# A norm's row kept on chip, keys and mask loaded later, and an output gain moved from VectorE to ScalarE's copy

## The reference

```
proj  = rms_norm(x) * norm_mix_g @ w_in            # recurrent group | q | k | v
y_r   = rwkv7_group(proj[..., :P_RWKV], ...)       # 8 heads x 64, delta-rule recurrence
o     = windowed attention over 2 chunks of history, softmax with a sink per head
y_a   = o * rsqrt(mean(o * o per head) + eps) * out_g            # attn_out_g, 512 values
x     = x + concat(y_r, y_a) @ w_out
t     = x * rsqrt(mean(x * x) + eps) * norm_ffn_g                # the second norm, 1024 values
# per row and head (8): scores with 2 x 128 keys, best 16 of the 16 x 16 sums, then
x     = x + sum over 128 experts of gate * gelu(down[e] . t) * up[e]
y     = rms_norm(x) * norm_final_g
```

## Time and profile before

| | before |
|---|---|
| median of 3 runs | 3971.74 us (3968.76 to 3976.06) |
| the profiled execution, its own time | 4006.36 us |
| its span, first to last instruction | 4004.6 us |
| mean granted clock of PE | 0.867 |
| busy share of PE, DVE, POOL, ACT | 78%, 72%, 38%, 35% |
| moved by DMA | 1424.83 MB, 356 GB/s over the span |
| of it the gathers' queue | 1223.91 MB |

### The profile page before, as it was taken

How to read it: one execution, slowest core, us unless ns; L and a number is a source line. 1 busy time by engine, 2 the same in 40 slices (tenths; PEclk the granted TensorE clock), 3 DMA queues, 4 the chain that set the end, 5 groups by cost and what they waited for, 6 DMA issues and landing times.

```text
span 4004.6 us, 43462 instructions
## 1 busy us (share of the span) xinstructions
PE 3116.8 (78%) x13880; PEld 1785.9 (45%) x13880; DVE 2889.2 (72%) x6010; ACT 1403.7 (35%) x4013; POOL 1534.6 (38%) x1323
## 2 busy tenths in 40 slices
PE   7999977778777877787778777877787778776556
PEld 4655645445443545354526353635363536352112
DVE  2221468779778886988698869886978698868775
ACT  2111133524343443334333524352425242523223
POOL 1333133334333433443344333442433244325554
PEclk9999988888798879887988798889878987899679
DMA  7234379999899999999999999999999999999998
GB/s 260 99 124 158 107 319 386 419 369 368 336 417 380 387 371 415 375 386 372 418 386 363 395 417 356 380 408 406 378 361 386 414 364 383 402 380 397 420 420 350
DMA packets 243305, 1424.83 MB, mean 356 GB/s; under 512 B 27763, under 2 KB 53107, under 8 KB 95606
## 3 DMA queue, kind: packets, MB, share of 16 engines
q0 software_dynamic: 170784, 1223.91, 75.6%
q1 hardware_dynamic: 61222, 180.44, 11.8%
q10 hardware_dynamic: 11072, 17.70, 1.3%
HBM read 1389.02 MB, written 34.17 MB: 355 GB/s over the span
## 4 chain that ended last, share of the span: by engine, by line
PE 31%; DVE 28%; DMA 12%; ACT 9%; issue 6%; POOL 1%; another core or an unknown queue 1%; DVEq 0%; POOLq 0%; PEldq 0%; SPq 0%; ACTq 0%
DVE ex_rows L1607 12%; PE mx_ps L1593 11%; DMA ex_rows<-experts,mx_expert 6%; PE mx_ps L1257 4%; DVE mx_acc L1617 2%; DMA mx_xs<-w_q 2%; DMA mx_fac<-w_q 2%; DMA mx_ex<-w_out 2%; PE mx_ps L1035 2%; ACT L1563 1%; PE mx_ps L1042 1%; PE mx_ps L999 1%; PE mx_ps L1240 1%; PE mx_ps L1038 1%; ACT L756 1%
## 5 line engine op out<-in xcount | busy, mean ns | idle before, releaser
L1552 POOL DMA_INDIRECT ex_rows<-experts,mx_expert x1152 | 1406.0, 1220 | 2084.1 <-PE mx_ps L1593 1202.6
L1593 PE MATMUL mx_ps<-ex_rows,ex_diag 128*128 128x512 f32 x2740 | 1506.1, 696 | 400.9 <-ACT ex_diag L1573 385.1
L1607 DVE CUSTOM_DVE_ANT_0 ex_rows<-ex_rows,mx_acc 128x1024 f32<-128x1024 f32 x1152 | 1371.8, 1221 | 151.8 <-DMA ex_rows<-experts,mx_expert 133.7
L1593 PEld LDWEIGHTS mx_ps<-ex_rows,ex_diag 128*128 128x128 f32 x2740 | 564.7, 219 | 1169.0 <-issue 1161.5
L1563 ACT ACTIVATE ex_coef<-ex_coef 128x1 f32<-128x1 f32 x1152 | 213.7, 200 | 1463.8 <-DVE ex_coef L1607 1450.1
L1617 DVE SCALAR_TENSOR_TENSOR mx_acc<-ex_rows,ex_coef,mx_acc 128x1024 f32<-128x1024 f32 x467 | 599.0, 1283 | 92.5 <-ACT ex_coef L1566 64.8
L1416 PE MATMUL mx_ps<-pj_w,pj_hT 128*128 128x432 f32 x768 | 292.5, 539 | 5.8 <-ACT mx_acc L1429 4.7
L1566 ACT ACTIVATE ex_coef<-ex_coef,mx_gate 128x1 f32<-128x1 f32 x1152 | 283.9, 284 | 10.6
L1573 ACT ACTIVATE ex_diag<-cn_ident,ex_coef 128x128 f32<-128x128 f32 x685 | 255.5, 394 | 10.7
L1416 PEld LDWEIGHTS mx_ps<-pj_w,pj_hT 128*128 128x128 f32 x768 | 146.8, 194 | 138.2 <-issue 135.5
L1563 ACT ACT_TABLE_LOAD x130 | 166.8, 1283 | 13.4 <-DVE ex_coef L1607 10.4
(11 more groups left out here) (316 smaller groups left out, 3978.9 us busy)
## 6 DMA issues: line engine op xcount, KB each, us to landing
mx_fac<-w_q SPq DMA_DIRECT2D x54, 512.0 KB
mx_ex<-w_out SPq DMA_DIRECT2D x36, 512.0 KB
mx_ex<-w_q SPq DMA_DIRECT2D x36, 512.0 KB
ex_rows<-experts,mx_expert POOLq DMA_INDIRECT x1152
mx_p_cur<-w_q SPq DMA_DIRECT2D x27, 512.0 KB
mx_xs<-w_q SPq DMA_DIRECT2D x27, 512.0 KB
proj_rows<-mx_acc ACTq DMA_DIRECT2D x48, 216.0 KB, 1.9
mx_fac<-w_out SPq DMA_DIRECT2D x18, 512.0 KB
```

The source lines that it names most:

```text
L1552: pool.indirect_dma_start(rows[:, g % RING, :], None, A["experts"], bass.IndirectOffsetOnAxis(expert[:, t % 2, s:s + 1], 0))\
L1593: last = pe.matmul(bank(6 + c), diag[:, diags.due(t, n) % DIAGS, :], up[:, r, c * 512:(c + 1) * 512], start=n == 0, stop=n == len(on_pe(t) ...
L1607: dve.tensor_tensor_reduce(out=down[:, r, :], in0=down[:, r, :], in1=tn[:, :], scale=1.0, scalar=0.0, op0=ALU.mult, op1=ALU.add, accum_out ...
```

## The change

The row of the second norm becomes a constant on chip: it is loaded once in `prepare` into a buffer of its own, and `route_sync` no longer loads it. The keys, values and mask of a prompt tile are loaded into the buffer `bkT`, after the last product that reads it, by `queries_sync` instead of `mix_sync`; their two buffers go. The gain of attention's output is no longer a row that DVE multiplies with: it is loaded as a 128 x 4 column table, and ACT applies it as a scale in its copy of the transposed `cat`, where a column of the output is a partition.

```
-    for name, at, n in (("r_k", RKC, RW), ("ln_w", LNW, RW), ("ln_b", LNB, RW), ("out_g", OUTG, RW),
+    for name, at, n in (("r_k", RKC, RW), ("ln_w", LNW, RW), ("ln_b", LNB, RW),
...
+        "out_g": sb("out_g", [P, RW // P]), "norm_ffn": sb("norm_ffn", [P, D]),
...
-             (C["iota"][:, :], row(A["iota"]).to_broadcast([P, NCAND]))]
+             (C["iota"][:, :], row(A["iota"]).to_broadcast([P, NCAND])), (C["out_g"][:, :], A["out_g_col"]),
+             (C["norm_ffn"][:, :], row(A["norm_ffn"]).to_broadcast([P, D]))]
...
-        gain = part(pqb, 0, (D,))
+        gain = C["norm_ffn"][:, :]
...
-            else:
-                sp.dma_start(m["kv"][:, :, :], proj[bass.ds(src, 2 * P), K0:P_TOTAL]
-                             .rearrange("(n p) c -> p n c", p=P)).then_inc(kv_in.sem, 16)
-                sp.dma_start(m["amask"][:, :], A["mask_prompt"][bass.ds(src, P), :]).then_inc(mask_in.sem, 16)
...
-        def queries_sync(sp, t, src):
+        def queries_sync(sp, t, m, src):
             sp.wait_ge(factors.sem, factors.due(t, 5))
             sp.dma_start(q_rows, proj[bass.ds(P + src, P), Q0:K0]).then_inc(q_in.sem, 16)
+            if not m["sample"]:
+                sp.wait_ge(n_out.sem, n_out.due(t, 1))
+                sp.dma_start(m["kv"], proj[bass.ds(src, 2 * P), K0:P_TOTAL]
+                             .rearrange("(n p) c -> p n c", p=P)).then_inc(kv_in.sem, 16)
+                sp.dma_start(m["amask"], A["mask_prompt"][bass.ds(src, P), :]).then_inc(mask_in.sem, 16)
...
-            link(dve.tensor_tensor(h3(y[:, :]), h3(y[:, :]), per_head(ast[:, 7, :]), ALU.mult))
-            dve.tensor_tensor(cat[:, RW:D], y[:, :], B(OUTG, RW), ALU.mult).then_inc(cat_ready.sem, 1)
+            dve.tensor_tensor(h3(cat[:, RW:D]), h3(y[:, :]), per_head(ast[:, 7, :]), ALU.mult).then_inc(cat_ready.sem, 1)
...
-            sp.dma_start(gain, row(A["norm_ffn"]).to_broadcast([P, D])).then_inc(gain_in.sem, 16)
...
-            act.activation(aT, blocks(banks(0, 2)), ACT.Copy).then_inc(mT_ready.sem, 1)
+            act.activation(aT[:, 0:4, :], blocks(bank(0)), ACT.Copy)
+            for k in range(4):
+                last = act.activation(aT[:, 4 + k, :], ps[:, 1, k * P:(k + 1) * P], ACT.Copy, scale=out_g[:, k:k + 1])
+            last.then_inc(mT_ready.sem, 1)
...
-            dve.wait_ge(gain_in.sem, gain_in.due(t, 16))
...
-                "kv": sb2("kv", [P, 2, 256]), "amask": sb2("amask", [P, 2 * P]), "keyT": part(pqk, 8 * P, (2 * P,)),
+                "kv": part(bkT, 2 * P, (2, 256)), "amask": part(bkT, 0, (2 * P,)), "keyT": part(pqk, 8 * P, (2 * P,)),
```

More of the change, by code:

```diff
@@ L44 @@
 DECAY = -math.exp(-0.5)
-RKC, LNW, LNB, OUTG, SINK = 0, RW, 2 * RW, 3 * RW, 4 * RW
-BC_COLS = 4 * RW + HEADS
+RKC, LNW, LNB, SINK = 0, RW, 2 * RW, 3 * RW
+BC_COLS = 3 * RW + HEADS
 NEG = -1e30
 W0_ROW, A0_ROW, KK_ROW = 32, 64, 96
-DVE_LINKS = 54
-DVE_LINKS_SAMPLE = 63
+DVE_LINKS = 53
+DVE_LINKS_SAMPLE = 62
 ROUTE_LINKS = 37
@@ L507, in mix_and_route @@
         qT = part(pqb, 2 * RW, (PAIRS, P))
+        out_g = C["out_g"]
         lora = part(fac, 0, (2 * LORA + GLORA,))
         big = part(pqb, 0, (16, P))
-        gain = part(pqb, 0, (D,))
+        gain = C["norm_ffn"][:, :]
         s12 = part(pqk, 0, (16, P))
@@ L600, in mix_and_route @@
         dve_link = flag("mix_dve_link", DVE_LINKS, DVE_LINKS_SAMPLE)
-        gain_in = flag("gain_in", 16)
         x_in = flag("xr_in", 16)
@@ L670, in mix_sync @@
                 sp.dma_start(m["kv"][:, SAMPLES, :], proj[bass.ds(P + src, P), K0:P_TOTAL]).then_inc(kv_in.sem, 16)
-                sp.dma_start(m["amask"][:, :], A["mask_sample"]).then_inc(mask_in.sem, 16)
+                sp.dma_start(m["amask"], A["mask_sample"]).then_inc(mask_in.sem, 16)
                 for b in range(SAMPLES):
@@ L929, in mix_vector @@
                 link(dve.tensor_tensor(m["sc"][d], bank(m["sc_bank"][d])[:, 0:width],
-                                       m["amask"][:, :], ALU.add))
+                                       m["amask"], ALU.add))
                 link(dve.tensor_reduce(ast[:, 0, h:h + 1], m["sc"][d], AX.X, ALU.max))
@@ L1389, in mix_and_route @@
                 "column": lambda n: 2 * (n % 4) + n // 4,
-                "kv": sb1("kv", [P, NK, 256]), "amask": sb1("amask", [P, 3 * P]), "keyT": keyT_s[:, :],
+                "kv": sb1("kv", [P, NK, 256]), "amask": sb1("amask", [P, 3 * P])[:, :], "keyT": keyT_s[:, :],
                 "sc": [late[:, n, :] for n in range(2)], "prT": [late[:, 2 + n, :] for n in range(2)],
@@ L1477, in _ @@
                     sp.dma_start(dst, src).then_inc(copied.sem, 16)
-                queries_sync(sp, 0, SEQ)
+                queries_sync(sp, 0, m, SEQ)
                 sp.wait_ge(s_ready.sem, SAMPLES)
@@ L1659, in _ @@
                         store_y(sp, t - 1)
-                    queries_sync(sp, t + 1, t * P)
+                    queries_sync(sp, t + 1, m, t * P)
                     route_sync(sp, t + 1, t * P)
@@ L1797 @@
         "k_k": a["rwkv_k_k"][0], "k_a": a["rwkv_k_a"][0], "r_k": a["rwkv_r_k"][0].reshape(-1),
-        "ln_w": a["rwkv_ln_w"][0], "ln_b": a["rwkv_ln_b"][0], "out_g": a["attn_out_g"][0],
+        "ln_w": a["rwkv_ln_w"][0], "ln_b": a["rwkv_ln_b"][0], "out_g_col": np.ascontiguousarray(a["attn_out_g"][0].reshape(RW // P, P).T),
         "sinks": a["attn_sinks"][0], "norm_ffn": a["norm_ffn_g"][0], "norm_final": a["norm_final_g"],
```

## The result

| | before | after |
|---|---|---|
| median | 3967.95 us (6 runs, 3944.72 to 3976.06) | 3936.65 us (6 runs, 3914.16 to 3960.31) |
| ratio | | 0.992, 95% interval 0.9893 to 0.9948 |
| profiled execution, span | 4004.6 us | 3938.1 us |
| mean granted clock of PE | 0.867 | 0.877 |
| moved by DMA | 1424.83 MB | 1420.37 MB |

The change gave 31 us, 0.8% (by the interval of the ratio 21 to 42).

What follows compares the result with a forecast made beforehand. No engine alone was taken to set the end: the chain passes between PE, DVE, ACT and DMA. Seven tiles at -0.73 us plus 0.1 us gave -5.0 us, from 3971.7 to 3966.7 us; the range was 3952 to 3978.

Steps and rivals of the forecast that it cites:

- Constants: Loads of constants: norm_ffn and the column come, out_g's row goes; worth nothing, without DMA slack about 1 us once.
- the sum: Whole kernel: 7 x -0.73 + 0.1 = -5.0 us, giving 3966.7 us; chance 0.45.
- out_g leaves DVE: End of attention: one DVE multiply goes, so PE is released 0.73 us earlier in each of seven prompt tiles.
- out_g on ACT: ACT's copy of transposed cat: 0.83 us longer, hidden in seven tiles; costs 0.1 us in the first prompt tile.
- What follows passes through: w_out's weight stream after attention: its wait moves with the earlier issue, so the 0.73 us pass through.
- The wash: Rival at w_out's blocks: bytes ahead hold the stream, so 0.73 us are waited away; 3971.7 us, chance 0.22.
- The sign that the prediction names: Profile after, prompt tiles: the tile period is 0.7 us shorter.
- The gain row stays on chip: Nine 512 KB loads of the second norm's row go, eight in prompt tiles; valued at nothing.
- The bound of -9.9 us: Most that the spared gain loads in prompt tiles could give, if DVE's waits for gathers reach the chain.
- Keys and mask later: Keys and mask loads moved after the last product reading bkT: nothing, with bounds of +7.4 and -7.4 us.
- The clock as a rival: Rival at w_out's first matmuls: PE's clock rises too late, each of seven tiles loses 3.2 us; 3989.0 us, chance 0.10.

Runs made afterwards that it cites:

- keys_only: Kernel before with only the later load of keys, values and mask into bkT; ring at byte 127968: 3971.38 us, ratio 0.9989.
- keys_ring_1024: keys_only with 32 unused bytes right ahead of the ring of expert rows, which then starts at byte 128000: 3947.94 us, ratio 0.9948.
- the other pairs: Kernels with PE's idle 3.82 us filled: ring at a multiple of 256 (3896.77, 3898.29, 3899.91 us) against ring off it (3920.33, 3925.61, 3927.26 us).
- The four multiplies added: Kernel before with PE's idle gap filled, and DVE's multiply by out_g made five times: 3939.16 us, ratio 0.992, against 3920.33 us with the gap filled alone.
- the filled pairs: Gap-filled kernels with against without out_g's move: ring off 256, 3925.61 against 3920.33 and 3927.26 us; on it, 3896.77 and 3899.91 against 3898.29.
- filled_gap_after: Changed kernel with 16 identity multiplications in PE's idle time at the end of the triangular solve: 3896.77 us, ratio 0.9821 to the kernel before.
- keys_filled_ring_1024: Kernel before with keys and mask loaded later, PE's idle gap filled and the ring at byte 128000: 3898.29 us, ratio 0.983.
- filled_gap_outg: Kernel before with PE's idle gap filled and only out_g's move to ACT; ring at byte 129024: 3899.91 us, ratio 0.9835.

## Why the prediction was wrong

**The failed step** is the one headed "Constants": "norm_ffn (512 KB) and the column come, the row of out_g (256 KB) goes, ahead of a stretch in which the DMA is at 0.14. Nothing". I counted what the edited constants cost to load, and not where they put what is allocated behind them. The ring moved from byte 131040 to 130048, from a multiple of 32 to one of 1024, and that is worth some 16 to 23 us of the 31 (by `keys_only` and `keys_ring_1024`; the other pairs give 21 to 26). No rival held it, so the range missed too. That the time fell as forecast is no support for the sum: most of the fall came from the ring. The trace of before could have warned of it in one way only: the last stage is bound by the DMA at 420 GB/s, a rate that I took as given. The two allocations, printed side by side, would have shown the move.

A rule of the Trainium skill bears on it: DMA: Bandwidth & Descriptors, section How a descriptor splits into AXI transactions, says, by the vendor's account, that a transaction must start at a multiple of 256 bytes, so that the first one of a descriptor that does not start there begins at the multiple below, and the bytes ahead of the start are fetched for nothing. It says so of what a descriptor reads. Here it was the address written that changed, and the runs show the same 256 bytes for it: 421.4 GB/s at a multiple of 128, 427.1 at one of 256. That this is the mechanism was not shown.

Step by step:

- **out_g leaves DVE: right at its place, its worth open.** Forecast 0.73 us in each of seven tiles; PE's wait shrank from 7.3 to 6.6 us. The four multiplies added give 0.59 us for each 0.73, 4.7 us in all; with the ring unaligned the changed kernel keeps 0.23% (9 us, between 1 and 17); but the filled pairs show nothing of the move. The 5.0 us lie within what can't be told apart.
- **out_g on ACT: right, a little dear.** From the first copy's start to the last one's end are 1.63 us, where I took 1.85; they end 1.75 us before w_out starts. In the first prompt tile w_out waits 1.72 us for ACT instead of 1.11, 0.6 us against the 0.73 gained: -0.1 instead of +0.1 us. The prediction had the busy time make the move a loss of 0.1 us a tile: measured, ACT's copies are 0.61 us longer (1.63 instead of 1.02) and DVE's multiply of 0.69 us is gone, so there is no loss even by busy time.
- **What follows passes through: right for time added.** The wash would have given 3920 to 3926 us with five multiplies; it was 3939.16. For time taken away it is not shown. The sign that the prediction names, a tile period 0.7 us shorter, can't be read: from choice to choice the periods are 368 to 394 us in the profile after and 382 to 396 in the one before.
- **The gain row stays on chip: right, nothing that can be told from no change.** Without the load 0.9991. The bound of -9.9 us was not needed.
- **Keys and mask later: right, likewise.** 0.9989.
- **The clock as a rival: right that it costs, wrong where.** I looked for it at w_out, and L1244's first eight matmuls take 3.59 us, where they took 3.56. It falls at the end of the triangular solve, in kernels with and without the change. It adds scatter to the times, and the filled pairs show that the gain does not come from it.

After the ring's 16 to 23 us and nothing to 9 for the move, up to 15 of the 31 us have no cause shown; the intervals of the ratios are as wide as that. Why the clock holds after the same idle 3.82 us in some tiles and falls in others stays open.

## What to carry to other kernels

An edit that adds, drops or resizes a buffer moves every buffer allocated behind it: print the start address of each large DMA destination before and after, and compare two kernels only when these agree in their place within 256 bytes, or say that they don't. Keep a ring that gathers write to on a multiple of 256 bytes; here 32 unused bytes were worth 0.4 to 0.6%, half to three quarters of what a three-part change had seemed to bring. And look for short idle times of PE ahead of a serial stretch: filling one of 3.8 us with useless products gave 1.3%, more than the whole change, and with the change 1.8% (`filled_gap_after`, 3896.77 us, the fastest kernel here beside `keys_filled_ring_1024` and `filled_gap_outg`).

## What the runs showed of the hardware

- Gathers of 8 KB rows into SBUF ran at 420 GB/s with the destination at a multiple of 32 bytes and no more, 421.5 at one of 64 or 128, and 427 at one of 256 or 1024. The median time of one 8 KB packet in that stage was 313 ns before and 309 ns after.
- On VectorE and ScalarE the same instructions took the same times at either address: DVE's dots 1222 ns in the changed kernel, 1220 in a tile of the kernel before; ACT's diagonals 394 ns in both the earlier trace rows.
- Behind the same idle time of 3.82 us of PE the granted clock was 0.90 on average in one tile and 0.71 in another, and the recurrence took 47.5 or 60.0 us.
